# Latent attention: turned probabilities and values kept whole, even and odd key tiles multiplied into two halves of the partitions

## What is computed

```python
def _mla_attention(q_nope, q_rope, k_nope, k_rope, v):
    seqlen = q_nope.shape[1]
    scale = (MLA_NOPE + MLA_ROPE) ** -0.5
    outs = []
    for blk in range(seqlen // Q_BLOCK):
        q0 = blk * Q_BLOCK
        kend = q0 + Q_BLOCK
        s = (jnp.einsum('bqhd,bkhd->bhqk', q_nope[:, q0:kend], k_nope[:, :kend])
             + jnp.einsum('bqhr,bkr->bhqk', q_rope[:, q0:kend], k_rope[:, :kend]))
        s = s.astype(jnp.float32) * scale
        mask = jnp.arange(kend)[None, :] <= (q0 + jnp.arange(Q_BLOCK))[:, None]
        s = jnp.where(mask, s, -jnp.inf)
        p = jax.nn.softmax(s, axis=-1).astype(v.dtype)
        outs.append(jnp.einsum('bhqk,bkhd->bqhd', p, v[:, :kend]))
    return jnp.concatenate(outs, axis=1)
```

## Time and profile before

| | |
|---|---|
| median of 3 runs | 2650.02 us (2649.67 to 2657.27) |
| the profiled execution, its own time | 2650.2 us |
| its span | 2648.4 us |
| mean granted TensorE clock | 0.996 |
| PE busy | 2569.6 us (97%) |
| DVE, ACT, POOL busy | 1651.3 us (62%), 1055.4 us (40%), 1146.2 us (43%) |
| shares of the chain that ended last | PE 83%, DVE 9%, ACT 5%, issue 3% |

### The profile page before, as it was taken

How to read it: one execution, slowest core, us unless ns; L and a number is a source line. 1 busy time by engine, 2 the same in 40 slices (tenths; PEclk the granted TensorE clock), 3 DMA queues, 4 the chain that set the end, 5 groups by cost and what they waited for, 6 DMA issues and landing times.

```text
span 2648.4 us, 32612 instructions
## 1 busy us (share of the span) xinstructions
PE 2569.6 (97%) x12496; PEld 2055.2 (78%) x12496; DVE 1651.3 (62%) x1992; ACT 1055.4 (40%) x1502; POOL 1146.2 (43%) x1422
## 2 busy tenths in 40 slices
PE   8999999999999999999999999989999999999998
PEld 7877878687787887877776777757888888888886
DVE  6636663768648658567777566674455565555556
ACT  3627881436305315225366656673201111111132
POOL 4633344532432432432432222224565567655653
PEclk9999999999999999999999999999999999999999
DMA  3111002222112212111220010102111111111312
GB/s 139 48 52 32 17 25 93 83 66 96 56 48 73 64 48 73 64 56 64 107 92 24 25 32 24 33 16 103 52 53 45 52 56 56 50 46 48 121 47 80
DMA packets 44820, 156.32 MB, mean 59 GB/s; under 512 B 4928, under 2 KB 5312, under 8 KB 44672
## 3 DMA queue, kind: packets, MB, share of 16 engines
q1 hardware_dynamic: 31392, 110.11, 12.7%
q10 hardware_dynamic: 13280, 44.17, 4.7%
HBM read 141.55 MB, written 12.71 MB: 58 GB/s over the span
## 4 chain that ended last, share of the span: by engine, by line
PE 83%; DVE 9%; ACT 5%; issue 3%; POOL 1%; ACTq 0%; DVEq 0%; POOLq 0%
PE PS L787 37%; PE PS L1461 13%; PE PS L1487 10%; PE PS L1117 4%; PE PS L1024 3%; PE PS L1509 2%; PE PS L1150 1%; PE PS L923 1%; PE PS L1160 1%; PE PS L1372 1%; PE PS L1154 1%; PE PS L937 1%; DVE sb_softplus L2965 1%; PE PS L1333 1%; ACT mla_p L1686 1%
## 5 line engine op out<-in xcount | busy, mean ns | idle before, releaser
L640 POOL CAST w_hi<-w_stage 128x1024 fp32r<-128x1024 f32 x130 | 145.5, 1120 | 1047.9 <-PE PS L787 757.0
L643 POOL TENSOR_TENSOR w_lo<-w_stage,w_hi 128x256 fp32r<-128x256 f32 x520 | 496.7, 987 | 10.4
L787 PE MATMUL PS<-XH,w_hi 128*128 128x512 f32 x1216 | 385.3, 398 | 7.5 <-ACT ssd_z L1901 3.3
L787 PE MATMUL PS<-XL,w_hi 128*128 128x512 f32 x1216 | 376.4, 391 | 0.0
L787 PE MATMUL PS<-XH,w_lo 128*128 128x512 f32 x1216 | 375.6, 390 | 0.0
L787 PEld LDWEIGHTS PS<-XH,w_hi 128*128 128x128 f32 x1216 | 222.9, 188 | 61.3 <-issue 9.7
L787 PEld LDWEIGHTS PS<-XL,w_hi 128*128 128x128 f32 x1216 | 228.8, 188 | 48.9
L787 PEld LDWEIGHTS PS<-XH,w_lo 128*128 128x128 f32 x1216 | 228.8, 188 | 48.8
L714 POOL TENSOR_TENSOR w_lo<-w_stage,w_hi 128x256 fp32r<-128x256 f32 x260 | 220.1, 854 | 0.0
L710 POOL CAST w_hi<-w_stage 128x256 fp32r<-128x256 f32 x260 | 126.3, 489 | 184.9 <-PE PS L1461 107.6
L1461 PE MATMUL PS<-raw_hi,w_hi 128*128 128x512 f32 x512 | 158.0, 390 | 0.0
(11 more groups left out here) (466 smaller groups left out, 5541.3 us busy)
## 6 DMA issues: line engine op xcount, KB each, us to landing
w_stage<-w SPq DMA_DIRECT2D x202, 512.0 KB, 3.3
ssd_sum_rows<-sums_kept ACTq DMA_DIRECT2D x32, 512.0 KB, 3.7
H<-x_t ACTq DMA_DIRECT2D x8, 512.0 KB, 8.1
pj_kept<-ple_proj_tiles ACTq DMA_DIRECT2D x8, 512.0 KB, 2.6
h_kept<-H ACTq DMA_DIRECT2D x8, 512.0 KB, 3.4
H<-h_kept ACTq DMA_DIRECT2D x4, 1024.0 KB, 5.5
out_t<-out_tiles SPq DMA_DIRECT2D x16, 256.0 KB, 2.1
x_again<-x_t ACTq DMA_DIRECT2D x12, 256.0 KB, 3.0
```

What stands on the lines that cost most here:

```text
L640: nc.gpsimd.tensor_copy(w_hi[:, slot, :, :], w_stage[:, slot, :, :]).then_inc(s_w_hi, 1)
L643: nc.gpsimd.tensor_tensor(w_lo[:, slot, k:k + 2, :], w_stage[:, slot, k:k + 2, :], w_hi[:, slot, k:k + 2, :].bitcast(F32), ALU.subtract).t ...
L787: mm = nc.tensor.matmul(outs[:, half, :], wt[:, slot, k, :], a[:, k - first, half * HB:(half + 1) * HB], start=(k == whole[0] and wt is w_ ...
```

## The change

The values and the turned probabilities are no longer split. ACT's `chunk_hi` is gone from all ten places of a head, and DVE's `chunk_lo` becomes `chunk_copy`, a plain copy out of PSUM at the same place in DVE's list; it waits for the transposes itself. `v_lo` is gone, and `v_hi` writes the whole values in fp32. `chunk_values` now multiplies plain fp32: the stationary operand is one key tile by 64 columns; the even key tile of the chunk (e = 0) goes to PSUM partitions 0 to 63, the odd one (e = 1) to 64 to 127, for each of the two query tiles (q) of 128 columns. On the diagonal the masked quarter is left out. In chunk 9 the first query tile has one key tile only; it is cut in two halves of 64 keys, one for each half of the partitions. `low_part` and `add_low` stay as they are and now add even and odd key tiles.

```diff
             def chunk_values(u, c):
                 (i, p), n = MLA_CHUNKS[c], NCH * u + c
                 if c == 0:
-                    pe.wait_ge(s_kvl, 2 * u + 4)
+                    pe.wait_ge(s_kvh, 2 * u + 4)
                 if c in (0, 7) and u:
                     pe.wait_ge(s_add, 2 * u - (c == 0))
-                pe.wait_ge(s_tlo, n + 1)
+                pe.wait_ge(s_tcp, n + 1)
                 b, q0 = 6 + i // 2, i % 2 * 2 * P
-                for src in (PTH, PTL):
+                late = int(p == i)
+                for q in range(2):
                     for e in range(2):
-                        late = P if e and p == i else 0
-                        mm = nc.tensor.matmul(PS[:, b, q0 + late:q0 + 2 * P], VM[:, u % 2, 2 * p + e, :],
-                                              src[:, n % 4, 2 * P * e:2 * P * (e + 1) - late],
-                                              start=(c in (0, 7) and e == 0 and src is PTH), stop=True, skip_group_check=True)
+                        o, cols_ = slice(64 * e, 64 * e + 64), slice(q0 + P * q, q0 + P * (q + 1))
+                        if q >= e * late and (i or q):
+                            at_ = 2 * P * e + P * (q - e * late)
+                            mm = nc.tensor.matmul(PS[o, b, cols_], VM[:, u % 2, 2 * p + e, :], PT[:, n % 4, at_:at_ + P],
+                                                  start=(c in (0, 7) and q == 0), stop=True, skip_group_check=True)
+                        elif i == 0:
+                            nc.tensor.matmul(PS[o, b, cols_], VM[o, u % 2, 0, :], PT[o, n % 4, 0:P], start=False, stop=True, skip_group_check=True)
                 mm.then_inc(s_pv, 1)
...
-            def chunk_hi(u, c):
-                n, wide = NCH * u + c, chunk_width(c)
-                act.wait_ge(s_tp, n + 1)
-                if n >= 4:
-                    act.wait_ge(s_pv, n - 3)
-                nc.scalar.activation(PTH[:, n % 4, 0:wide], PS[:, 4 + n % 2, 0:wide], ACT.Copy).then_inc(s_thi, 1)
...
-            def v_lo(u):
-                dve.wait_ge(s_kvh, 2 * u + 4)
-                v.tensor_tensor(VM[:, u % 2, :, 64:128], PS[:, 2 * mla_pair(("v", u)), :].rearrange("p (t d) -> p t d", d=64),
-                                VM[:, u % 2, :, 0:64].bitcast(F32), ALU.subtract).then_inc(s_kvl, 1)
...
-            def chunk_lo(u, c):
+            def chunk_copy(u, c):
                 n, wide = NCH * u + c, chunk_width(c)
-                dve.wait_ge(s_thi, mla_high("chunk", u, c))
-                v.tensor_tensor(PTL[:, n % 4, 0:wide], PS[:, 4 + n % 2, 0:wide], PTH_f[:, n % 4, 0:wide], ALU.subtract).then_inc(s_tlo, 1)
+                dve.wait_ge(s_tp, n + 1)
+                if n >= 4:
+                    dve.wait_ge(s_pv, n - 3)
+                v.tensor_copy(PT[:, n % 4, 0:wide], PS[:, 4 + n % 2, 0:wide]).then_inc(s_tcp, 1)
```

More of the change, by code:

```diff
@@ L160 @@
 NCH = len(MLA_CHUNKS)
-MLA_HIGHS = []
-for _u in range(MLA_H):
-    if _u:
-        MLA_HIGHS += [("chunk", _u - 1, 9), ("low", _u - 1, 0)]
-    MLA_HIGHS += [("chunk", _u, _c) for _c in range(9)] + [("low", _u, 1)]
-MLA_HIGHS += [("chunk", MLA_H - 1, 9), ("low", MLA_H - 1, 0)]
 MLA_RING = [("q", 0), ("k", 0), ("v", 0)]
@@ L173 @@
 MLA_TURN = {_key: _n for _n, _key in enumerate(MLA_RING)}
-def mla_high(*key):
-    return MLA_HIGHS.index(key) + 1
 def mla_pair(key):
@@ L479, in program @@
         s_tp = sem("mla_chunk_turned")
-        s_thi = sem("mla_chunk_hi_made")
-        s_tlo = sem("mla_chunk_split")
+        s_thi = sem("mla_part_copied")
+        s_tcp = sem("mla_chunk_copied")
         s_pv = sem("mla_value_products")
@@ L2441, in _ @@
             k_lo(0)
-            v_lo(0)
             v.memset(SM[:, 5, 0:1], 0.0).then_inc(s_evac[1], MLA_H // 2)
@@ L2451, in _ @@
                 if u:
-                    chunk_lo(u - 1, 9)
+                    chunk_copy(u - 1, 9)
                 invert(u, 1)
@@ L2467, in _ @@
                     k_lo(u + 1)
-                chunk_lo(u, 3)
+                chunk_copy(u, 3)
                 neg_max(u, 5)
-                chunk_lo(u, 4)
+                chunk_copy(u, 4)
                 invert(u, 4)
-                chunk_lo(u, 5)
+                chunk_copy(u, 5)
                 invert(u, 5)
-                if more:
-                    v_lo(u + 1)
                 neg_max(u, 6)
-                chunk_lo(u, 6)
+                chunk_copy(u, 6)
                 neg_max(u, 7)
-                chunk_lo(u, 7)
+                chunk_copy(u, 7)
                 invert(u, 6)
                 invert(u, 7)
-                chunk_lo(u, 8)
+                chunk_copy(u, 8)
             u = MLA_H - 1
             add_low(u, 1)
-            chunk_lo(u, 9)
+            chunk_copy(u, 9)
             add_low(u, 0)
```

38 lines of the change are left out of this document (13 added, 25 removed).

## The result

The changed kernel takes 2663.64 us (median of 11 runs, 2661.01 to 2667.76), the kernel before 2651.77 us (median of 11 runs on the same chip, 2649.67 to 2657.27). The ratio is 1.0043, interval 1.0035 to 1.0051: slower by 12 us. The profiled execution took 2663.68 us with a span of 2661.9 us, against 2648.4 us of span before.

What follows compares the result with a forecast made beforehand. TensorE was taken as the bound, busy 24.02 of a middle head's 24.85 us, but with waits. Five middle heads at +1.25 us and 1.25 for three others gave 7.5 on 2650.2: 2658 us, range 2649 to 2666.

Steps and rivals of the forecast that it cites:

- Copies: ACT loses ten rounding copies per head, some 5.5 of 20.18 us; DVE loses one `v_lo`, about 0.69.
- The products: Value products per head: two overlapping pairs 0.44 us a chunk; with edges, nine counted chunks 6.7 against 4.66, +2.05 us.
- rival B: Value products: the halves do not overlap, a full chunk takes 0.88 us; 28 us more, 2686 in all; chance 0.04.
- The edges: Entering and leaving each block of half-column products costs 0.29 us, making 0.73 a chunk; chunk 9 has 0.14 more.
- The waits: TensorE's 1.87 us of waits per head: 0.8 stay as one wait for `k_lo` ahead of score rows 5, others go.
- The sum: Per middle head +2.05 minus 0.8 of waits, +1.25 us; five of these plus three other heads at 0.42: 7.5 us.
- the forecast case: Whole kernel: edges paid, about half of the waits gone; 2658 us, own range 2652 to 2664; chance 0.72.
- Rival C: DVE, alone between transposes and value products, becomes late: a further 0.5 us per head, 2662 us and more; chance 0.07.
- Rival A: Value-product blocks: edges cost much less, a block with edges below 0.61 us; not slower, 2638 to 2646; chance 0.17.

Runs made afterwards that it cites:

- the kernel with old products: Against the kernel before: one rounded DVE copy, none on ACT, four full-width fp32r products kept, low parts left out; 2646.73 us, ratio 0.9979.
- The kernel without halves: Changed kernel with plain fp32 products of full width, 128 columns of weights (64 zero), 256 streamed, chunk 9 not cut; 2665.21 us, ratio 1.0048.
- the execution with no low clock in its attention: Profiled execution of the changed kernel with 128 instead of 64 columns streamed in the values projection; median 2661.24 us, ratio 1.0032.
- five blocks with the waits left in: Changed kernel with value products of chunks 0-1, 2-3, 4-5, 6 and 7-9 grouped, five blocks a head instead of ten; 2665.1 us, ratio 1.0044.
- the same five blocks without one of the waits: The five-block version of the changed kernel with `k_lo` ahead of the maximum of score rows 4; 2663.87 us, ratio 1.0042.

## Why the prediction was right, point by point

The forecast was 2658 us, slower by 8 us; it was 2663.64, slower by 12. The direction and the mechanism were right, and the size came out short by about what the clock took in the attention, of which no step spoke.

- **Copies.** ACT was put at 14.5 us busy per head and has 15.94. The ten copies do last 5.5 us taken one by one, but ACT's instructions overlap: in the head of the earlier trace rows their durations add up to 23.0 us where ACT is busy 20.18, in the head after to 17.5 where it is busy 15.94. A duration taken off a busy time took off too much; ACT's busy time fell by 4.2. Nothing hung on it. That DVE's copy costs what the subtraction did holds: 679 ns against 687, and 692 was taken. The copies pay 0.7 us a head, as the kernel with old products shows, near the 0.8 of the sum.
- **The products.** They were put at +2.05 us a head and came to 2.1, as the kernel with old products and one copy shows (26.24 - 24.16). Two pairs were put at 0.44 us. A block from its first product to what follows takes 0.59, the steps inside it 0.11 to 0.16 apart with the last at 0.20; that contains the 0.05 of the first pair and the 0.10 of the last, as in the earlier trace rows. The kernel without halves took 0.92, so the halves do overlap, and rival B is out, for diagonal chunks also: those take 0.58 and lose nothing.
- **The edges.** Forecast for a chunk with both edges 0.73 us: 0.12 ahead (0.09 forecast), 0.59 inside, 0.05 behind makes 0.76. Chunk 9 was put at 0.73 + 0.14 = 0.87 with its edges; it takes 0.73 inside, about 0.10 ahead and 0.05 behind, 0.88. The row of the state-space layer carried over to a block with two pairs. Two readings beside it were off, and neither changed the outcome: seven of the ten blocks follow a mask product (chunks 0, 2, 3, 5, 6, 7 and 8), not six, and of the old chunks, put at 0.54 and 0.49, chunk 1 took 323.18 - 322.70 = 0.48 us and chunk 9 took 341.94 - 341.54 = 0.40, so the old products cost a little less than the 5.2 us. The Trainium skill, "TensorEngine Tiling (Array Packing)", section Key Properties, had it that changing the tiling mode drains TensorE; the kernel without halves, where neither edge appears, agrees.
- **The waits.** 0.8 us were to remain ahead of score rows 5 behind `k_lo`, and all others to go. The wait is 0.85, and in the undisturbed head there is no other of note. The cause is shown by a run: with `k_lo` ahead of `neg_max` the wait is gone.
- **The sum.** A middle head was put at 26.1 and takes 26.23. Five middle heads at 1.25 us and three other heads at 0.42 came to 7.5 us, and blocks and waits made 7.9; the execution with no low clock in its attention has 7.7 more span than before. That the sum fits better than its terms is luck in part: the middle heads took more (7.1 us instead of 6.25), the three others less (0.6 for the first, 0.1 each for the last two, instead of 1.25).
- **The step that is missing** is TensorE's clock. The forecast took every term at 2.4 GHz, as the earlier trace rows had it, and the changed kernel spent some 10 us of the heads and 7 ahead of them at 1.2 GHz, 4.5 us and 1.35 in time. Together these 5.85 us are about the 5.6 us by which the forecast was missed. That the result still lies at the upper end of the forecast case's own range (2652 to 2664) is luck: that range was drawn for edges and waits, not for the clock.
- **Rival C** is out: TensorE waits for the chunk copies nowhere in a middle head.
- **Rival A** is out: it was to decide under 0.61 us for a block with its edges, and a block with its edges is 0.76.

**What stays open.** That products on halves bring the low clock in behind a head's values projection rests on seven of eight profiled executions against none of four; if it were chance which of the twelve have it, so clear a split would come once in 99 times. By what way they do it is not shown. That streaming 128 columns in the projection takes it away again is not shown either. It rests on two profiled executions with none in 14 heads, against 14 in the 35 heads of the five profiled executions whose kernels differ from them only in these products or their place (3, 3, 3, 3 and 2). Counted by heads this would hardly be chance, but heads of one execution are not independent. Counted by executions, supposing the seven alike, chance would make the two without a fall just these two once in 21 times. With the other three kernels on halves (0, 2 and 7 falls) three of ten executions have none, and chance gives just these two among them once in 15 times. Why the profiled execution of five blocks with the waits left in had none inside its heads, and the same five blocks without one of the waits had one in each, is not explained. Nor was it tried to fill other stretches.

## What to carry to other kernels

Products on two halves of the columns pay per block, not per product: a block of two pairs came to 0.76 us with its edges against 0.58 for the four fp32r products it replaced with theirs, and a block of five and a half pairs came out about level. Before shortening an engine's work, look which chain ends the wait behind it: here the order of two neighbouring DVE instructions brought 0.86 us a head, the loss of ACT's ten copies 0.7. Where blocks were taken together, keep apart those that fill time beside such a chain.

## What the runs showed of the hardware

- In the kernels on halves TensorE's clock fell to 1.2 GHz inside the heads, 3.4 us at a time (once 6.8), and ahead of each of these 23 falls the profile counts TensorE as busy in all of the last 3 us. The busy share of the profile does not tell where they come. One stretch of 3.4 us costs a head 1.5 to 1.6 us. Elsewhere idle time stands ahead of some falls: before the one at 526.1 us in the kernel before, TensorE is busy for 1.2 of 3 us.
- The values projection's products cost the same with 64 and 128 streamed columns: 24 of them in 2.78 and 2.80 us. The added columns took no time, and in the two profiled executions no stretch at the low clock followed.
- Plain fp32 products on half the columns made the mask product ahead of a block last 0.16 us instead of 0.04, the last step inside it 0.20 where the others are 0.11 to 0.16, and the transposes behind it 0.41 instead of 0.36. With the same format at full width the mask product lasts 0.07 and the transposes are as before.
